# One x layout for both layers of the second block, and products of 512 columns issued as 256-column halves

## The chip, the cores and the metric

The kernel runs on one core of a Trainium2 chip. The metric is the device time of one execution in microseconds (us); smaller is better. Engines are named as the profile names them: PE is TensorE (PEld its weight loads), DVE is VectorE, ACT is ScalarE, POOL is GpSimd, SP is SyncE.

## The reference

Two transformer blocks, one behind the other, on 256 tokens of 1024 features in fp32. The first block (a recurrence with retention, a sparse attention, two feed-forward layers) is not touched in its code. The second block has two layers, and its first layer works on 512 rows: the 256 tokens of x ("now") and 256 tokens of a context. Its second layer takes the 256 tokens as queries and all 512 rows as keys. What the change touches is every product of the normed and modulated h with a weight matrix in these two layers:

```python
def _layer(x, xc, ...):
    h = _rms(x, norm_w) * (1.0 + sc[:, None, :]) + sh[:, None, :]
    hc = _rms(xc, norm_w) * (1.0 + sc_c) + sh_c
    aq, ak, av, az, dq, dk, dv, dz, bf, bz, cu, cv, cz = _split_in(h @ w_in)
    aqc, ... = _split_in(hc @ w_in)
    ...
    y = _merge(h, (o_a, o_d, o_b, o_c), (az, dz, bz, cz), w_br, w_merge, b_merge, w_out)

def _merge(h, outs, gates, w_br, w_merge, b_merge, w_out):
    yb = jnp.stack([o * jax.nn.silu(z) for o, z in zip(outs, gates)], axis=2)
    y = jnp.einsum('bnrw,rwd->bnrd', yb, w_br)
    g = jax.nn.sigmoid(h @ w_merge + b_merge).reshape(b, n, N_BRANCH, D_MODEL)
    return jnp.sum(g * y, axis=2) @ w_out
```

## The kernel before

**Products in three parts.** Each fp32 operand is kept as a high part of type float32r and a low part with the rest. A product of one 128 x 128 block of a weight with a block of h is three matmuls (`product`, L321): weight high by x high (L329), weight high by x low (L330), weight low by x high (L331). Each matmul instruction carries its own weight load, so three loads go with three matmuls, though the first two load the same block. A result tile of 128 features is a group of eight products, k = 0 to 7, accumulated in one PSUM bank of 512 fp32 columns: 24 matmuls. `features` (L333) issues such a group. `rows` (L341) issues the turned form, in which x is the loaded operand and 256 columns of the weight are streamed (L326 to L328).

**Where x lies.** `both` ("XX" in the profile) holds x high and x low, 4096 columns each (eight blocks k of 512 columns: NOW is 0 to 256, CTX is 256 to 512). There are two views of it. `XX0` (L146) has the high part at column 0 and the low part at column 4096. `XX` (L147) is "shifted": the high part starts at column HI = 48 and the low part 4096 + 64 columns behind it, at 4096 + LO with LO = 112. `XH` and `XL` are the two halves of the shifted view. The first block and layer 1 of the second block use the shifted view, layer 0 uses `XX0`. In front of `ring`, `X` and `arena` there are small unused tensors (L130, L140) that set where the large ones start.

```python
HI, LO = 48, 112
def shifted(v, n):
    return v[:, HI:HI + 2 * (n + LO - HI)].rearrange("p (s q) -> p s q", s=2)[:, :, 0:n]
```

**Who fills x.** `adapted_vector` (L436) and `adapted_scalar` (L454) apply the norm, gain and shift: ACT writes the high part, DVE the low part, 256 columns at a time.

**Layer 0** (`Layer`, L2026 and L2048: NT = 512 rows). Its PE program is a fixed order written out by hand:
- `context_keys_tensor` (L2154): the keys and values of the 512 rows, in groups of 256 columns (features of CTX and NOW, and turned products);
- `queries_tensor` (L2125) and `outer_tensor` (L2359): ten groups of 512 columns; `rest_tensor` (L2377): four turned groups of 256;
- `layer_tensor` (L2692): attention in 16 units, between whose steps `inner_tensor` (L2423) puts single groups of 512 columns (`product_of`, six of them) and, through `gate` (L2484), the first two gate groups, each in two pieces of four k;
- the merge, through `block` (L2722): 30 more gate groups of 512 columns, between them the branch products (`branches` in the profile, K = 2) of 512 columns; then the out products (`merged`) of 512 columns.

So there are 10 + 6 + 2 + 30 = 48 groups of 512 columns of x in layer 0.

**Layer 1** (NT = 256) streams 256 columns of x at a time, but for `all_keys_tensor` (L2135), whose two key groups take all 512 rows in one matmul each, from the shifted view.

**Weights** arrive by DMA (SP queue) in halves of 512 KB into `stage`, ACT copies them to the high part (`high`, L250), DVE takes the rest to the low part (`low`, L258); PE waits for a half in `Chunk.arrive` (L284). ACT waits with a chunk until PE is done with the chunk two before it. Sequence of chunks: `FLOW`, one fixed list.

Of the kernel before, what the change touches and what calls it, by code (L numbers as in the profile page):

```python
# [17 lines left out]
HI, LO = 48, 112  # L18
# [99 lines left out]
def build(nc, A, out):  # L118
    ctx = ExitStack()
    with ctx:  # L120
# [22 lines left out]
            return v[:, HI:HI + 2 * (n + LO - HI)].rearrange("p (s q) -> p s q", s=2)[:, :, 0:n]  # L143

        both = sb("XX", 8448, F32R)
        XX0 = both[:, 0:8192].rearrange("p (s k n) -> p s k n", s=2, k=8)  # L146
        XX = shifted(both, 4096).rearrange("p s (k n) -> p s k n", k=8)  # L147
        XH, XL = XX[:, 0], XX[:, 1]
        WH = [sb(f"WH{i}", 2048, F32R)[:, :] for i in range(2)]
# [52 lines left out]
        NOW, CTX = slice(0, 256), slice(256, 512)  # L202
# [118 lines left out]
        def product(e, dst, w, k, cols, xh, xl, start, stop, turned=False):  # L321
# [8 lines left out]
            e.matmul(dst, wh, xl, start=False, stop=False)  # L330
            return e.matmul(dst, wl, xh, start=False, stop=stop)  # L331

        def features(e, dst, w, c, name, x=None, xs=NOW, parts=(XH, XL)):  # L333

            for k in range(8):
                if x:
                    x(k)
                last = product(e, dst, w, k, slice(c, c + 128), parts[0][:, k, xs], parts[1][:, k, xs], k == 0, k == 7)
            last.then_inc(*pe.tick(name))

        def rows(e, dst, w, t, cols, name, x=None, base=0, parts=(XH, XL)):  # L341
# [92 lines left out]


        def adapted_vector(e, p, src, gain, shift, inv, t, xs, hold=None):  # L436
            x = (XX0, XX)[p[1] == "1"]

            def low(k):
                e.wait_ge(*ac.of(f"{p}.xh{k}"))  # L440
                e.scalar_tensor_tensor(out=x[:, 1, k, xs], in0=t[:, k, :], scalar=shift(k), in1=x[:, 0, k, xs].bitcast(F32),
                                       op0=ALU.add, op1=ALU.subtract).then_inc(*ve.tick(f"{p}.x{k}"))

            for k in range(9):
                if k < 8:
                    e.scalar_tensor_tensor(out=t[:, k, :], in0=src[:, k, :], scalar=gain(k), in1=inv, op0=ALU.mult,
                                           op1=ALU.mult).then_inc(*ve.tick(f"{p}.t{k}"))
                    if k == 7 and hold:
                        banks.emptied(hold, ve)
                if k > 0:  # L450
                    low(k - 1)
                yield

        def adapted_scalar(e, p, shift, t, xs):  # L454
            x = (XX0, XX)[p[1] == "1"]
            for k in range(8):
                e.wait_ge(*ve.of(f"{p}.t{k}"))
                e.activation(x[:, 0, k, xs], t[:, k, :], ACT.Identity, bias=shift(k)).then_inc(*ac.tick(f"{p}.xh{k}"))
                yield
# [1563 lines left out]
        class Layer:  # L2023
            def __init__(self, l):
                self.l = l
                self.NT = 512 if l == 0 else 256  # L2026
                self.nt, self.NZ = self.NT // 128, 2 * self.NT
                self.Z = view(0, 8 * self.NT, "p (r a n) -> p r a n", r=4, a=2)
                a = self.tail = 8 * self.NT
                self.R = [view(a + 1536 * n, 1536, "p (a n) -> p a n", a=3) for n in range(2)]  # L2030
                self.V = view(a + 3072, 1024, "p (t b c) -> p t b c", t=4, b=2)
                a += 4096
                self.S3 = [view(a + 1536 * n, 1536, "p (a n) -> p a n", a=3) for n in range(2)]
                self.T3 = [view(a + n, 768, "p (a n) -> p a n", a=3) for n in (3072, 4864)]
                self.RX = [view(a + 3840 + 512 * n, 512, "p (t h d) -> p t h d", t=4, h=2) for n in range(2)]
                self.S = [view(a + 1024 * n, 1024) for n in range(3)]
                self.T = [view(a + 3072 + 1024 * n, 1024) for n in range(2)]

                self.ms, self.rs = [SM[:, 24 * n:24 * n + 24] for n in range(2)], [SM[:, 48 + 24 * n:72 + 24 * n] for n in range(2)]
                d, NZ = C("decay"), self.NZ  # L2040
                self.U = d[:, 0:NZ].rearrange("p (a n) -> p a n", a=2)
                self.VT = d[:, NZ:2 * NZ].rearrange("p (t c) -> p t c", t=self.nt)
                self.Fm = self.U
                self.ZZ = d[:, NZ:NZ + 512].rearrange("p (t a c) -> p t a c", t=2, a=2)
                self.nsink = MOD[:, 96:100]
                NT = self.NT
                self.M = view(4096, 8 * NT, **eight)
                x, hi, lo = (XX0, 0, 0) if l == 0 else (XX, HI, LO)  # L2048
                self.x = x[:, 0], x[:, 1]
                self.MH, self.ML = [v[:, at:at + 8 * NT].rearrange("p (k n) -> p k n", k=8) for v, at in ((mh, hi), (ml, lo))]  # L2050
                self.SG, self.T2 = [[d[:, NT * (2 * i + n):NT * (2 * i + n + 1)] for n in range(2)] for i in range(2)]
                z = [v[:, at:at + w * NT].rearrange("p (r a n) -> p r a n", r=w // 2, a=2)
                     for v, w, at in ((zh, 8, hi), (zl0, 4, lo), (zl1, 4, lo))]

                self.ZH, self.ZL = [z[0][:, i] for i in (1, 0, 2, 3)], [z[1 + i // 2][:, i % 2] for i in range(4)]
                self.units, self.at = [], []

                self.steps = ([1] * 18 + [0], [2, 1, 2, 2, 1, 2, 1, 1, 2, 1, 0])[l]
                sink, nsink = [v.rearrange("p (q h) -> p q h", q=2) for v in (P("sink", l * 4, 4), self.nsink)]
                for br in range(2):  # L2060
                    for it in range(self.nt):
                        for h in range(2):
                            k0 = 0 if it < 2 else 256
                            rate = self.rs[br][:, 8 + 4 * it + 2 * h:10 + 4 * it + 2 * h].rearrange("p (q h) -> p q h", q=2)
                            self.units.append(Unit(1, 512 - k0, 512, rate,
                                                   (causalM, beforeM)[it] if br == 1 and it < 2 else None, 128 * (1 - it),
                                                   (sink[:, :, h:h + 1], nsink[:, :, h:h + 1]) if br else None))
                            self.at.append((br, it, h, k0))
# [354 lines left out]
        def inner_tensor(e, flow, rings, L):  # L2423
            l, NT, nt, s = L.l, L.NT, L.nt, (6, 7)
            w = {}
# [58 lines left out]
            def gate(m, ks):  # L2484
# [3 lines left out]
                    tile(e, f"g{l}.{m}.0", 1, (5,)) if l + m == 0 else tile(e, f"g{l}.{m}.0", 2, (0, 2))  # L2488
                b = banks[f"g{l}.{m}.0"]
                for k in ks:  # L2490
                    t = product(e, b[:, 0:NT], w["merge"], 8 * m + k, slice(0, 128), L.x[0][:, k, 0:NT], L.x[1][:, k, 0:NT], k == 0,
                                k == 7)
                if ks[-1] == 7:
                    t.then_inc(*pe.tick(f"g{l}.{m}.0"))
                    if m == 1:
# [5 lines left out]
            wsp, n = ring_take(e, rings, 512, "p (g q) -> p g q", g=4)  # L2501
# [190 lines left out]
        def layer_tensor(e, flow, rings, L):  # L2692
# [29 lines left out]
            def block(dst, xh, xl, k, K, name):  # L2722
                nonlocal w, n
                if n % 16 == 0:
                    w = Chunk(flow, f"merge_{l}", n // 16, 16)
                t = product(e, dst, w, n % 16, slice(0, 128), xh, xl, k == 0, k == K - 1)
                if k == K - 1:
                    t.then_inc(*pe.tick(name))
                elif n % 16 == 15:
# [470 lines left out]
```

## Time and profile before

| what | value |
|---|---|
| time of three runs, median (lowest to highest) | 1361.29 us (1360.18 to 1363.97) |
| the profiled execution's own time | 1365.15 us |
| its span, first to last instruction | 1363.3 us |
| granted TensorE clock, mean | 1.000 |
| PE busy | 1344.2 us, 99% of the span, 10306 matmuls |
| PEld busy | 1200.5 us, 88%, 10306 weight loads |
| DVE, ACT, POOL busy | 790.6, 640.8, 160.1 us (58%, 47%, 12%) |
| chain that ended last | PE 88%, DVE 7%, ACT 3%, issue 1%, DMA 1% |

The page gives busy time by engine, the chain of work that ended last, and groups of instructions by line. Matmuls are pipelined: the duration of one (276 ns for 256 columns, 389 ns for 512) is longer than the distance from its start to the next start, which is what it costs. That distance is read from start times in the timeline, or from a stretch that holds nothing else: in it the profile counts the matmuls that touch the stretch, so that one costs (length + one duration) / count.

### The profile page before, as it was taken

To read this page: it belongs to the slowest core of one execution; us is meant where nothing else is said; L and a number is where in the kernel's file an instruction comes from. 1 tells how busy PE (TensorE), PEld (TensorE's weight loads), DVE (VectorE), ACT (ScalarE), POOL (GpSimd) and SP (SyncE) were. 2 spreads that over 40 slices of the span, in tenths; PEclk is the share of its full clock that TensorE was granted. 3 is DMA by queue.
4 is the path that set the end of the run, shared out by engine and by line. 5 is a ranking of instruction groups with operands and counts; after the bars stand their busy time and mean duration, and the time that the engine had idled before them with its cause. 6 is when DMAs were issued, how large, how long until landed. Compare 5 with 4: busy or idle time off the path is not lost.

```text
span 1363.3 us, 24540 instructions
## 1 busy us (share of the span) xinstructions
PE 1344.2 (99%) x10306; PEld 1200.5 (88%) x10306; DVE 790.6 (58%) x1239; ACT 640.8 (47%) x1126; POOL 160.1 (12%) x131
## 2 busy tenths in 40 slices
PE   9999999999999999999999999999999999999999
PEld 8989999999855899999987777888888888879999
DVE  6976666557767666655724567433333455775554
ACT  6645444444365554455433445323232345555442
POOL 0020111001300012110004000111011100301110
PEclk9999999999999999999999999999999999999999
DMA  8535767556597455665432210222222234414553
GB/s 319 186 124 185 229 226 256 188 186 217 186 336 267 150 190 191 199 197 173 140 115 94 93 56 32 93 93 93 93 93 95 92 122 144 147 61 153 194 186 124
DMA packets 60974, 215.43 MB, mean 158 GB/s; under 512 B 6720, under 2 KB 12736, under 8 KB 57408
## 3 DMA queue, kind: packets, MB, share of 16 engines
q1 hardware_dynamic: 56272, 206.59, 45.4%
q10 hardware_dynamic: 4592, 7.26, 1.5%
q8 instruction: 82, 1.34, 0.4%
q14 instruction: 28, 0.23, 0.1%
HBM read 208.59 MB, written 1.05 MB: 154 GB/s over the span
## 4 chain that ended last, share of the span: by engine, by line
PE 88%; DVE 7%; ACT 3%; issue 1%; DMA 1%; SPq 0%; POOL 0%; ACTq 0%; DVEq 0%; POOLq 0%
PE psum L329 24%; PE psum L330 23%; PE psum L331 23%; DVE WL L261 3%; PE psum L1246 3%; PE psum L1271 2%; PE psum L1409 2%; PE psum L326 1%; PE psum L327 1%; PE psum L328 1%; ACT WH L256 1%; PE psum L2714 1%; PE psum L1602 1%; DMA stage<-ab_in 1%; PE psum L1250 1%
## 5 line engine op out<-in xcount | busy, mean ns | idle before, releaser
L329 PE MATMUL psum<-XX,WH 128*128 128x256 f32 (+1 forms) x1912 | 584.7, 306 | 8.2 <-DVE WL L261 2.8
L331 PE MATMUL psum<-XX,WL 128*128 128x256 f32 (+1 forms) x1912 | 576.3, 301 | 0.0
L330 PE MATMUL psum<-XX,WH 128*128 128x256 f32 (+1 forms) x1912 | 576.3, 301 | 0.0
L261 DVE TENSOR_TENSOR WL<-stage,WH 128x1024 fp32r<-128x1024 f32 x332 | 397.1, 1236 | 254.9 <-ACT WH L256 254.7
L256 ACT ACTIVATE WH<-stage 128x1024 fp32r<-128x1024 f32 x332 | 333.4, 1052 | 330.1 <-PE psum L331 286.0
L329 PEld LDWEIGHTS psum<-XX,WH 128*128 128x128 f32 x1912 | 359.4, 188 | 39.7 <-issue 13.8
L331 PEld LDWEIGHTS psum<-XX,WL 128*128 128x128 f32 x1912 | 359.9, 188 | 15.9
L330 PEld LDWEIGHTS psum<-XX,WH 128*128 128x128 f32 x1912 | 358.8, 188 | 15.7 <-issue 0.5
L329 PE MATMUL psum<-hidden,WH 128*128 128x256 f32 x352 | 97.5, 277 | 0.0
L331 PE MATMUL psum<-hidden,WL 128*128 128x256 f32 x352 | 97.2, 276 | 0.0
L330 PE MATMUL psum<-hidden,WH 128*128 128x256 f32 x352 | 97.2, 276 | 0.0
L2883 POOL TENSOR_TENSOR arena<-arena,con 128x512 f32<-128x512 f32 (+1 forms) x48 | 43.0, 895 | 385.6 <-DVE con L2801 385.0
L1371 ACT ACTIVATE arena<-psum,SM 128x16 f32<-128x16 f32 (+3 forms) x144 | 67.6, 482 | 2.3 <-DVE SM L1303 2.3
L329 PEld LDWEIGHTS psum<-hidden,WH 128*128 128x128 f32 x352 | 66.1, 188 | 0.4 <-issue 0.4
L330 PEld LDWEIGHTS psum<-hidden,WH 128*128 128x128 f32 x352 | 66.1, 188 | 0.0
L331 PEld LDWEIGHTS psum<-hidden,WL 128*128 128x128 f32 x352 | 66.1, 188 | 0.0
L1197 POOL TENSOR_TENSOR arena<-arena,SM 128x512 f32<-128x512 f32 x22 | 42.6, 1936 | 182.1 <-ACT arena L1164 182.1
L1356 ACT ACTIVATE arena<-psum 128x512 f32<-128x512 f32 (+2 forms) x48 | 32.9, 685 | 61.8 <-PE psum L1271 57.0
L2801 DVE TENSOR_TENSOR con<-psum,con 128x512 f32<-128x512 f32 (+1 forms) x48 | 26.3, 555 | 57.8 <-ACT con L2641 29.8
L2641 ACT ACTIVATE con<-psum,par 128x512 f32<-128x512 f32 (+1 forms) x64 | 35.6, 574 | 43.9 <-PE psum L331 43.9
L1300 DVE TENSOR_REDUCE SM<-psum 128x2 f32<-128x1024 f32 (+4 forms) x48 | 41.8, 872 | 20.2 <-PE psum L1246 12.2
L326 PE MATMUL psum<-WH,XX 128*128 128x256 f32 x176 | 49.9, 283 | 0.4 <-DVE WL L261 0.4
(288 smaller groups left out, 1675.7 us busy)
## 6 DMA issues: line engine op xcount, KB each, us to landing
stage<-w SPq DMA_DIRECT2D x132, 512.0 KB, 4.6
stage<-merge SPq DMA_DIRECT2D x80, 512.0 KB, 4.5
ring<-ada SPq DMA_DIRECT2D x24, 1024.0 KB, 7.0
stage<-in SPq DMA_DIRECT2D x44, 512.0 KB, 4.5
stage<-ab_in SPq DMA_DIRECT2D x22, 512.0 KB, 5.8
stage<-nsa_in SPq DMA_DIRECT2D x20, 512.0 KB, 4.8
stage<-out SPq DMA_DIRECT2D x16, 512.0 KB, 4.2
stage<-ab_out SPq DMA_DIRECT2D x8, 512.0 KB, 4.7
```

What stands on the lines that cost most here:

```text
L256: e.activation(hi, raw, ACT.Copy).then_inc(s_hi, 1)
L261: e.tensor_tensor(lo, raw, hi.bitcast(F32), ALU.subtract).then_inc(s_lo, 1)
L326: e.matmul(dst, xh, wh, start=start, stop=False)
L329: e.matmul(dst, wh, xh, start=start, stop=False)
L330: e.matmul(dst, wh, xl, start=False, stop=False)
L331: return e.matmul(dst, wl, xh, start=False, stop=stop)
L1197: e.tensor_tensor(F.sg[c % 3], F.sg[c % 3], spread(RT, 2, 256), ALU.mult).then_inc(*gp.tick(f"{p}.gate{c}"))
L1246: t = e.matmul(v[:, q, h, :], query(h)[r], key[r], start=h == 0 or u.mask is None, stop=u.mask is None)
L1300: e.tensor_reduce(nm, scored(p, n, u), AX.X, ALU.max, negate=True).then_inc(*ve.tick())
L1371: e.activation(s[:, q, h, :], v[:, q, h, :], ACT.Exp, bias=nm[:, q, h:h + 1], scale=rate, accum_out=sm[:, q, h:h + 1]).then_inc(*ac.tick(f ...
L2641: e.activation(L.SG[n % 2], banks[f"g{l}.{m}.{i}"][:, 0:L.NT], ACT.Sigmoid, bias=P("b_merge", l * 32 + MERGED[i] * 8 + m)).then_inc(*ac.ti ...
L2883: e.tensor_tensor(L.M[:, m, :], L.M[:, m, :], L.T2[n % 2], ALU.add).then_inc(*gp.tick(f"u{l}.{n}"))
```

## The change

`XX0` goes away: layer 0 of the second block keeps x in the shifted view, like the rest of the program. Groups of 512 columns of x go through a new function, `by_halves`. It issues the first matmul of a group (k = 0, weight high by x high) and the last (k = 7, the same operands) with 512 columns; all others are issued as three for the NOW half and three for the CTX half (at k = 0 and k = 7 two for each, since the third is the wide one). A group is then 46 matmuls in place of 24: 2 of 512 columns and 44 of 256. It is used wherever 512 columns of x are streamed: in the 48 groups of layer 0 and in the two key groups of layer 1. The products of `branches` and of `merged` keep their addresses and their 512 columns. The last matmul of a group signals its end, as before.

```diff
         both = sb("XX", 8448, F32R)
-        XX0 = both[:, 0:8192].rearrange("p (s k n) -> p s k n", s=2, k=8)
         XX = shifted(both, 4096).rearrange("p s (k n) -> p s k n", k=8)
...
+        def by_halves(e, dst, w, at, cols, k):
+            wh, wl = w.hi[:, at, cols], w.lo[:, at, cols]
+            w.arrive(e, at)
+            if k == 0:
+                e.matmul(dst, wh, XH[:, k, 0:512], start=True, stop=False)
+            for v in (NOW, CTX):
+                if 0 < k < 7:
+                    e.matmul(dst[:, v], wh, XH[:, k, v], start=False, stop=False)
+                e.matmul(dst[:, v], wh, XL[:, k, v], start=False, stop=False)
+                t = e.matmul(dst[:, v], wl, XH[:, k, v], start=False, stop=False)
+            if k == 7:
+                t = e.matmul(dst, wh, XH[:, k, 0:512], start=False, stop=True)
+            return t
...
         def features(e, dst, w, c, name, x=None, xs=NOW, parts=(XH, XL)):
+            both = parts[0] is XH and xs.stop - xs.start == 512
             for k in range(8):
                 if x:
                     x(k)
-                last = product(...)
+                if both:
+                    last = by_halves(e, dst, w, k, slice(c, c + 128), k)
+                else:
+                    last = product(...)
...
         def adapted_vector(e, p, src, gain, shift, inv, t, xs, hold=None):
-            x = (XX0, XX)[p[1] == "1"]
+            x = XX
...
         def adapted_scalar(e, p, shift, t, xs):
-            x = (XX0, XX)[p[1] == "1"]
+            x = XX
...
-                x, hi, lo = (XX0, 0, 0) if l == 0 else (XX, HI, LO)
-                self.x = x[:, 0], x[:, 1]
+                hi, lo = (0, 0) if l == 0 else (HI, LO)
+                self.x = XH, XL
...
             def gate(m, ks):
-                    t = product(e, b[:, 0:NT], w["merge"], 8 * m + k, ...)
+                    if NT == 512:
+                        t = by_halves(e, b[:, 0:NT], w["merge"], 8 * m + k, slice(0, 128), k)
+                    else:
+                        t = product(e, b[:, 0:NT], w["merge"], 8 * m + k, ...)
...
             def block(dst, xh, xl, k, K, name):
-                t = product(e, dst, w, n % 16, slice(0, 128), xh, xl, k == 0, k == K - 1)
+                if K == 8 and NT == 512:
+                    t = by_halves(e, dst, w, n % 16, slice(0, 128), k)
+                else:
+                    t = product(e, dst, w, n % 16, slice(0, 128), xh, xl, k == 0, k == K - 1)
```

## Rows read from the trace of the kernel before

**Rows 1.** The page: the chain of waits by engine.

```profile
PE 88%; DVE 7%; ACT 3%; issue 1%; DMA 1%; SPq 0%; POOL 0%; ACTq 0%; DVEq 0%; POOLq 0%
```

**Rows 2.** Stretches of one kind of matmul (engine: busy us, xcount of instructions).

```profile
core 0: us, PE busy (x) PEld busy (x) DVE busy (x) ACT busy (x) POOL busy (x), PEclk, DMA share, GB/s
500.00:600.00 100.00, 100.00 (x885) 100.00 (x884) 62.07 (x73) 46.58 (x64) 19.83 (x10) 1.00 0.59 193
672.00:689.00 17.00, 17.00 (x144) 17.00 (x143) 10.76 (x26) 8.01 (x14) 0.00 (x0) 1.00 0.11 38
900.00:1050.00 150.00, 150.00 (x664) 124.20 (x663) 49.27 (x53) 44.77 (x55) 20.06 (x18) 1.00 0.30 99
1137.00:1146.50 9.50, 9.50 (x43) 7.59 (x42) 5.66 (x11) 7.49 (x13) 0.00 (x0) 1.00 0.42 142
1240.00:1340.00 100.00, 100.00 (x851) 100.00 (x850) 52.79 (x68) 48.48 (x71) 18.81 (x28) 1.00 0.58 189
```

**Rows 3.** Groups by form, 663 to 1113 us, PE (xcount | busy, mean ns | idle).

```profile
L329 PE MATMUL psum<-XX,WH 128*128 128x512 f32 x384 | 151.3, 394 | 0.0
L331 PE MATMUL psum<-XX,WL 128*128 128x512 f32 x384 | 149.6, 390 | 0.0
...
L326 PE MATMUL psum<-WH,XX 128*128 128x256 f32 x64 | 18.1, 283 | 0.0
...
L329 PE MATMUL psum<-XX,WH 128*128 128x256 f32 x32 | 9.3, 291 | 0.0
```

**Rows 4.** Groups by form, 1126 to 1175 us, PE.

```profile
L329 PE MATMUL psum<-XX,WH 128*128 128x512 f32 x16 | 6.3, 395 | 0.0
```

**Rows 5.** Chain of waits, 774 to 777 us (start us, us, what).

```profile
774.85 0.87 PE psum L1271 x8
```

**Rows 6.** Timeline of PE, first stretch at shifted addresses, 15 us (start us, us).

```profile
14.63 0.39 PE L329 MATMUL psum<-XX,WH 128*128 128x256 f32 x1 [0.77 <-DVE WL L261]
14.85 0.28 PE L330 MATMUL psum<-XX,WH 128*128 128x256 f32 x1
...
16.78 0.28 PE L329 MATMUL psum<-XX,WH 128*128 128x256 f32 x1
```

**Rows 7.** Timeline of PE behind two transposes, 1160 us (start us, us).

```profile
1160.06 0.37 PE L329 MATMUL psum<-XX,WH 128*128 128x256 f32 x1
1160.27 0.28 PE L330 MATMUL psum<-XX,WH 128*128 128x256 f32 x1
...
1161.18 0.28 PE L329 MATMUL psum<-XX,WH 128*128 128x256 f32 x1
```

**Rows 8.** Timeline of PE behind a wait, 317 us.

```profile
316.69 0.36 PE L329 MATMUL psum<-XX,WH 128*128 128x256 f32 x1
316.88 0.28 PE L330 MATMUL psum<-XX,WH 128*128 128x256 f32 x1
...
317.83 0.28 PE L329 MATMUL psum<-XX,WH 128*128 128x256 f32 x1
```

**Rows 9.** Timeline of PE behind attention scores, layer 0, 777 us.

```profile
776.71 0.50 PE L329 MATMUL psum<-XX,WH 128*128 128x512 f32 x1
777.05 0.40 PE L330 MATMUL psum<-XX,WH 128*128 128x512 f32 x1
...
778.66 0.39 PE L331 MATMUL psum<-XX,WL 128*128 128x512 f32 x1
```

**Rows 10.** Timeline of PE, start of layer 1's merge, 1230 us.

```profile
1230.15 0.39 PE L329 MATMUL psum<-branches,WH 128*128 128x256 f32 x1
1230.37 0.28 PE L330 MATMUL psum<-branches_low,WH 128*128 128x256 f32 x1
...
1231.31 0.28 PE L329 MATMUL psum<-branches,WH 128*128 128x256 f32 x1
```

**Rows 11.** Waits of PE, 663 to 1113 us (us in total, times, longest).

```profile
PE psum L1901 <- DVE SM L1927: 0.6, 1, 0.6
PE psum L2458 <- DVE arena L2775: 0.2, 1, 0.2
```

More of the change, by code:

```diff
@@ L337, in features @@
                     x(k)
-                last = product(e, dst, w, k, slice(c, c + 128), parts[0][:, k, xs], parts[1][:, k, xs], k == 0, k == 7)
+                if both:
+                    last = by_halves(e, dst, w, k, slice(c, c + 128), k)
+                else:
+                    last = product(e, dst, w, k, slice(c, c + 128), parts[0][:, k, xs], parts[1][:, k, xs], k == 0, k == 7)
             last.then_inc(*pe.tick(name))
@@ L2490, in gate @@
                 for k in ks:
-                    t = product(e, b[:, 0:NT], w["merge"], 8 * m + k, slice(0, 128), L.x[0][:, k, 0:NT], L.x[1][:, k, 0:NT], k == 0,
-                                k == 7)
+                    if NT == 512:
+                        t = by_halves(e, b[:, 0:NT], w["merge"], 8 * m + k, slice(0, 128), k)
+                    else:
+                        t = product(e, b[:, 0:NT], w["merge"], 8 * m + k, slice(0, 128), XH[:, k, NOW], XL[:, k, NOW], k == 0, k == 7)
                 if ks[-1] == 7:
```

## The prediction

> **What bounds the kernel now.** I read the chain of waits first. PE carries 88% of the chain that ended last [rows 1], and the three lines of `product` are nearly all of that, so what counts is the distance from one matmul's start to the next. In layer 0 of the second block PE waits for other engines 0.8 us in 450 us [rows 11]: nothing hides a longer product, and nothing eats a shorter one. The granted clock is 1.00, the level of 2.4 GHz, in every stretch read [rows 2]; PE's work stays as dense after the change, so I change nothing there. DMA is busy 0.30 of the time in the merge, ACT 45 and DVE 49 us of 150 [rows 2]: weights are no bound, now or at 5% either way.
>
> Then I took stretches that hold only one kind of matmul and divided. Length plus one duration, over the count, gives [rows 2]:
> - 256 columns, shifted, 500 to 600 us (feed-forward): 100.28/885 = 113.3 ns;
> - 256 columns, shifted, 1240 to 1340 us (merge of layer 1): 100.28/851 = 117.8 ns;
> - 256 columns, unshifted, 672 to 689 us: 17.28/144 = 120.0 ns;
> - 512 columns, unshifted, 900 to 1050 us (merge of layer 0): 150.39/664 = 226.5 ns;
> - 512 columns, shifted, 1137 to 1146.5 us (keys of layer 1): 9.89/43 = 230 ns; one matmul fewer in the count would make 235, and I take 233.
>
> Two things are to be seen. A 512-column matmul at `XX0`'s addresses costs exactly two of the fast 256-column ones (2 x 113.3 = 226.6). And at shifted addresses the same instruction has two levels, 113.3 and 117.8, each of them kept for 100 us and more. Which one a stretch takes is set at its start, behind an interruption: eight steps from 1160.27 take 0.91 us (114) [rows 7], eight from 316.88 take 0.95 us (119) [rows 8], eight from 1230.37 take 0.94 us (118), and that one keeps the slow level through the merge of layer 1 [rows 10, 2]. I counted the stretches of at least 12 such matmuls at shifted addresses: 50, from the first at 15 us (17 steps in 1.93 us, 114 ns) [rows 6] to the last at 1230 us [rows 10]; 26 end at the fast level and 24 at the slow one. I see no line, operand or half of x that goes with either. So for a stretch in a new place it is close to a coin.
>
> What makes the 256-column form cost over 106.7 ns (256 columns at 2.4 GHz) is most likely its weight load: eight transposes of only 128 columns, each with a load, take 0.87 us, 109 ns each [rows 5], although they stream half as much, and PEld is busy in the whole of both 256-column stretches but in 124 of 150 us beside 512 columns [rows 2].
>
> **The change, part by part.**
>
> 1. Groups of layer 0. 384 matmuls of 512 columns by each of three lines [rows 3], that is 1152/24 = 48 groups, each 24 x 226.6 = 5438 ns. After: 44 halves and 2 wide ones. The wide ones are now shifted: 233 each, 466 (bounds 226.6 and 235). The halves: at the fast level 44 x 113.3 = 4985, the group 5451, **+13 ns**, +0.6 us in 48 groups. At the slow level 44 x 117.8 = 5183, the group 5649, **+211 ns**, +10.1 us. Below, the nearest row is the 109 ns of a 128-column matmul: 44 x 109 = 4796, the group 5262, -176 ns, -8.4 us. No row shows a 256-column product under 113.3, so this is the bound and not the value. I take the fast level: in a group the halves follow a wide matmul, whose 233 ns leave its successor's load done long before, so that they start without a late load, and that is how the two longest stretches (feed-forward) run on; but this is the weak step.
>
> 2. Entry into a group. A 512-column stretch behind the attention's matmuls needs some steps to settle: seven steps from 777.05 take 1.61 us, 230 each in place of 226.6, and the first takes 0.34 us [rows 9]. 18 groups of layer 0 lie there. After, the first step is wide again and as dear, and only two wide steps are left to be unsettled; the halves cost 0.5 to 1 ns over for some eight steps [rows 7]. 18 x (24 to 50 ns) saved against 48 x (0 to 20 ns) spent: zero, bounds -0.9 and +1.0 us.
>
> 3. The 256-column products of layer 0 (keys, values, turned ones): 64 by each of L326 to L328, 32 by each of L329 to L331 [rows 3], 288 together, unshifted at 120.0, shifted at 113.3 or 117.8: -1.9 or -0.6 us, I take the middle, **-1.3 us**.
>
> 4. The two key groups of layer 1, 16 matmuls by each line [rows 4]: 24 x 233 = 5592 before, 5451 or 5649 after: **-0.3 us** or +0.1.
>
> 5. 50 x 22 = 1100 more matmuls and loads. The price of a load is in the distances above. Instruction fetch: no row of layer 0 shows PE waiting for it, and the 256-column stretches already issue at this rate. Zero. No wait is added or moved; ACT and DVE write x in the same order at the new columns, zero as well, hidden as before by PE's work.
>
> Here a page speaks against the change. The Trainium skill, "TensorE: Matmul & The Clock Gate", section "Back-to-back issue gap", gives 262 cycles for 256 columns and 518 for 512, a fixed cost of about 2.5 ns for each matmul. By it a split costs 2.5 ns: an estimate from that page is 50 x 22 x 2.5 ns = 2.8 us slower, 1363. The trace doesn't agree: it shows 2 x 113.3 against 226.5, no fixed cost to be saved by width.
>
> Sum: +0.6 + 0 - 1.3 - 0.3 = -1.0 us. The profiled execution took 1365.15 us with a span of 1363.3, the median of the runs is 1361.29 and they spread over 3.8 us; two levels that differ by 4.5 ns in the some 1100 matmuls of layer 1's merge alone (851 in 100 us, and it lasts 130 us: 4.9 us) can make such a spread. I put the -1.0 to the median: **1360.3 us**. A measurement of this kernel can tell about 0.3%, 4.1 us, from no change.
>
> **The rivals.**
>
> - *The halves run at the slow level.* Place: the 48 groups of layer 0. For it: 24 of 50 stretches, and the stretch nearest in kind, layer 1's merge, which starts out of a row of attention matmuls and mixes x and branch products [rows 10, 2]. Against it: both feed-forward stretches, 100 us and more at 113.3. Price: +10.1 - 0.6 + 0.1 = +9.6, so 1370.9 us. It decides from where the mean of the 2112 halves passes 113.3 + (4.1 + 1.0) us/2112 = 115.7 ns. Chance 0.25.
> - *Each group falls to a level of its own*, since two wide matmuls interrupt the halves in every group. Half of them slow: +5.3 - 1.3 - 0.1 = +3.9, so 1365.2 us. Chance 0.15, evenly on both sides of the 0.3%.
> - *Faster, the halves under 113.3.* Two halves behind one wide matmul could run nearer to the load's own 109 ns [rows 5]: -8.4 - 1.3 - 0.6 = -10, 1351 us. Against it: no stretch of 256 columns does. Chance 0.10.
> - *Faster, layer 1 gets the fast level.* Its merge starts afresh behind attention; 1100 products by 4.5 ns are -4.9 us, with the forecast -5.9, so 1355.4 us. For it: that level is taken at a start, and the starts will fall otherwise. Against it: the spread of the runs suggests that this coin is thrown in every run, so that the median has it in already. Chance 0.13.
> - *The change does nothing at all* (the forecast without its small gains, 1361.3) can't be told from the forecast and shares its chance, 0.37 together.
>
> **How the numbers follow.** Same: 0.37 and half of 0.15, 0.44. Faster by over 0.3%: 0.10 + 0.13 = 0.23, and a little for bounds of both: 0.24. Slower by over 0.3%: 0.25 + 0.07 = 0.32. The range must take the slow level in at one end, 1371, and at the other the case of layer 1, with part of the way to the load's bound: 1353. The likeliest case's own range, from the bounds of terms 1 to 4, is 1358 to 1363.
>
> **What would show it.** In the profile after: 11406 matmuls; no 512-column matmul on XX but 100 (two in each of 50 groups). In a stretch of layer 0's merge, a group of gates plus its branch products takes 5451 + 6 x 226.6 = 6811 ns if the forecast holds, 7009 at the slow level, against 6798 before. The stretch from 672 to 689 us should show 113.3 or 117.8 and not 120. PE's weight loads should be busy nearly all of the merge, not 0.83 of it. The forecast is wrong if the halves' mean distance lies above 115.7 or under 112, or if waits of PE for weights (DVE, L261) turn up in layer 0.

## The result and the profile after

| | before | after |
|---|---|---|
| median of the first comparison (4 runs each) | 1361.85 us | 1369.62 us (1368.41 to 1372.2) |
| ratio, 95% interval | | 1.005 [1.0029, 1.0071] |
| second comparison (26 and 10 runs) | 1367.07 us | 1368.52 us, 0.9999 [0.9974, 1.0024] |
| third comparison (23 and 12 runs) | 1367.43 us | 1370.67 us, 1.0022 [0.9999, 1.0045] |
| span of the profiled execution, again, a third time | 1363.3, 1363.3 us | 1366.6, 1367.8, 1363.3 us |

The forecast was 1360.3 us, 1.0 us less than before. In the first comparison the changed kernel is slower, by 0.3 to 0.7%, and the other two can't tell it from no change. By how much it is slower, the medians tell badly (7.8, 1.5 and 3.2 us); the profiles tell it well. From the last matmul on `hidden` (the input of the feed-forward layer's second product, the last work of the first block) to the first on `early` (the input of layer 1's first products), a stretch that is layer 0 and a few us around it, the kernel before takes 444.7 us in both of its profiles, the changed one 448.3, 448.5 and 448.7: **+3.6 to +4.0 us**. Two executions, 1480.1 us of the kernel before and 1658.4 us with the addresses alone, ran at a mean granted clock of 0.85 and 0.75 and are in no ratio.

The engines' busy time and the chain of waits, from the page of the changed kernel:

```profile
PE 1347.2 (99%) x11406; PEld 1247.5 (91%) x11406; DVE 790.8 (58%) x1239; ACT 641.0 (47%) x1126; POOL 160.0 (12%) x131
...
PE 88%; DVE 7%; ACT 3%; issue 1%; DMA 1%; SPq 0%; POOL 0%; ACTq 0%; DVEq 0%; POOLq 0%
```

1100 matmuls and loads more, PEld at 91% of the span in place of 88, and the chain as before [rows 1]: the change did what it says, and PE bounds the kernel as it did.

Groups by form, 663 to 1117 us, PE (xcount | busy, mean ns of one | idle):

```profile
L341 PE MATMUL psum<-XX,WH 128*128 128x256 f32 x768 | 207.0, 278 | 0.0
...
L340 PE MATMUL psum<-XX,WH 128*128 128x256 f32 x576 | 160.7, 279 | 0.0
L328 PE MATMUL psum<-branches,WH 128*128 128x512 f32 x64 | 25.2, 394 | 0.0
...
L337 PE MATMUL psum<-XX,WH 128*128 128x512 f32 x48 | 20.1, 418 | 0.0
L344 PE MATMUL psum<-XX,WH 128*128 128x512 f32 x48 | 18.8, 391 | 0.0
L325 PE MATMUL psum<-WH,XX 128*128 128x256 f32 x64 | 17.9, 279 | 0.0
```

In layer 0, 48 groups with a wide matmul at the start (L337), one at the end (L344), and 44 halves (768 + 768 + 576 = 2112 in all) stand where three lines had 384 wide ones each [rows 3] (L342, with 768 as well, is left out above). The branch products are the same 192, but their mean duration went up from 389 to 391 ns to 392 to 394.

Stretches of the changed kernel (engine: busy us, xcount):

```profile
core 0: us, PE busy (x) PEld busy (x) DVE busy (x) ACT busy (x) POOL busy (x), PEclk, DMA share, GB/s
673.00:689.00 16.00, 16.00 (x142) 16.00 (x141) 10.35 (x25) 7.20 (x12) 0.00 (x0) 1.00 0.05 16
...
900.00:1050.00 150.00, 150.00 (x1130) 142.73 (x1129) 49.27 (x53) 44.11 (x54) 19.98 (x18) 1.00 0.28 96
1236.00:1336.00 100.00, 100.00 (x852) 100.00 (x851) 55.22 (x71) 49.06 (x72) 16.78 (x25) 1.00 0.56 188
```

Divided as before (length plus one duration, over the count), 673 to 689 gives 16.28/142 = 114.6 ns where the unshifted addresses gave 120.0 [rows 2]: this part of the change works. In the merge, the timeline over three neighbouring groups (start us, us; L337 is the first matmul of a group, L344 its last) shows what the groups cost:

```profile
865.54 0.39 PE L337 MATMUL psum<-XX,WH 128*128 128x512 f32 x1
...
870.96 0.39 PE L344 MATMUL psum<-XX,WH 128*128 128x512 f32 x1
871.19 0.39 PE L328 MATMUL psum<-branches,WH 128*128 128x512 f32 x1
...
872.57 0.39 PE L337 MATMUL psum<-XX,WH 128*128 128x512 f32 x1
872.80 0.28 PE L341 MATMUL psum<-XX,WH 128*128 128x256 f32 x1
...
878.03 0.39 PE L328 MATMUL psum<-branches,WH 128*128 128x512 f32 x1
...
879.41 0.39 PE L337 MATMUL psum<-XX,WH 128*128 128x512 f32 x1
...
886.44 0.39 PE L337 MATMUL psum<-XX,WH 128*128 128x512 f32 x1
```

From the first wide matmul at 872.57 to the next group's at 879.41 are 6.84 us, a gate group and six branch matmuls. The group before it began at 865.54 and took 7.03 to 872.57, and so does the one behind it (879.41 to 886.44). The expected values were 6811 ns for a fast group and 7009 for a slow one, against 6798 before. So **both levels are there, by turns**: the 30 groups of the merge take 5.457 and 5.648 us alternately, without one exception, and all three profiles show the same order. Behind a slow group the closing wide matmul takes 233 ns, behind a fast one 226 (870.96 to 871.19: 0.23). From the first branch product to the first on `merged` the merge takes 210.9 us in all three profiles, before 206.9 in both.

Where the 4.0 us of the merge go, from the distances of all its matmuls: the halves of 15 slow groups, 15 x 44 x 4.4 ns = 2.9; the halves of the 15 fast groups, 0.2 us over 113.3 while they settle; 60 wide x products at 231.1 in place of 226.7, 0.3; and 192 branch products, whose addresses and width didn't change, at 230.7 in place of 227.6, 0.6.

### The profile page after: what moved, and what is told of

Read it like the earlier page. It is cut to its first block, busy times and chain, and to the rows that moved or that the text cites. A ratio compares the mean times of both kernels' runs of the same rounds, so it can differ in the third digit from the quotient of the medians.

```text
span 1366.6 us, 26740 instructions
## 1 busy us (share of the span) xinstructions
PE 1347.2 (99%) x11406; PEld 1247.5 (91%) x11406; DVE 790.8 (58%) x1239; ACT 641.0 (47%) x1126; POOL 160.0 (12%) x131
## 4 chain that ended last, share of the span: by engine, by line
PE 88%; DVE 7%; ACT 3%; issue 1%; DMA 1%; SPq 0%; POOL 0%; ACTq 0%; DVEq 0%; POOLq 0%
PE psum L328 17%; PE psum L329 17%; PE psum L330 17%; PE psum L341 7%; PE psum L342 7%; PE psum L340 5%; DVE WL L260 3%; PE psum L1264 3%; PE psum L1289 2%; PE psum L1427 2%; PE psum L325 1%; PE psum L327 1%; PE psum L326 1%; ACT WH L255 1%; PE psum L2734 1%
## 5 line engine op out<-in xcount | busy, mean ns | idle before, releaser
L328 PE MATMUL psum<-XX,WH 128*128 128x256 f32 x1512 | 427.0, 282 | 8.4 <-DVE WL L260 3.4
L329 PE MATMUL psum<-XX,WH 128*128 128x256 f32 x1512 | 419.9, 278 | 0.0
L330 PE MATMUL psum<-XX,WL 128*128 128x256 f32 x1512 | 419.9, 278 | 0.0
L328 PEld LDWEIGHTS psum<-XX,WH 128*128 128x128 f32 x1512 | 284.0, 188 | 19.3 <-issue 10.0
L330 PEld LDWEIGHTS psum<-XX,WL 128*128 128x128 f32 x1512 | 284.9, 188 | 0.0
L329 PEld LDWEIGHTS psum<-XX,WH 128*128 128x128 f32 x1512 | 283.6, 188 | 0.5 <-issue 0.5
L341 PE MATMUL psum<-XX,WH 128*128 128x256 f32 x800 | 215.6, 278 | 0.0
L342 PE MATMUL psum<-XX,WL 128*128 128x256 f32 x800 | 215.4, 278 | 0.0
L340 PE MATMUL psum<-XX,WH 128*128 128x256 f32 x600 | 167.4, 279 | 0.0
L342 PEld LDWEIGHTS psum<-XX,WL 128*128 128x128 f32 x800 | 150.3, 188 | 2.2
L341 PEld LDWEIGHTS psum<-XX,WH 128*128 128x128 f32 x800 | 150.3, 188 | 1.5
L340 PEld LDWEIGHTS psum<-XX,WH 128*128 128x128 f32 x600 | 113.6, 189 | 1.2 <-issue 1.2
```

The lines of the kernel that those rows point to most:

```text
L328: e.matmul(dst, wh, xh, start=start, stop=False)
L340: e.matmul(dst[:, v], wh, XH[:, k, v], start=False, stop=False)
L341: e.matmul(dst[:, v], wh, XL[:, k, v], start=False, stop=False)
L342: t = e.matmul(dst[:, v], wl, XH[:, k, v], start=False, stop=False)
```

## The experiments

All start from one of the two kernels. "Merge" is the time from layer 0's first branch product to its first on `merged`; before 206.9, after 210.9. "Layer 0" is from the last matmul on `hidden` to the first on `early`; before 444.7, after 448.3 to 448.7. "Tail" is from layer 1's first branch product to the end of the span; before 133.1 twice, after 133.1, 133.1 and 128.3. "Fast" and "slow" are the two levels, 113.3 and 117.8 ns for 256 columns at shifted addresses. A train is a row of halves without a wide matmul in it; the wide ones or the 256-column ones settle when their distances have come down to an even value after an interruption.

### Both kernels again

> The kernel before, unchanged, for a second profile. Theory A (the level of a stretch of 256-column products follows from the fixed order of PE's instructions in front of it): the stretches show the same levels as in the first profile where PE waits for nobody, feed-forward layers 113.3 ns, layer 1's merge 117.8 ns. Theory B (a coin thrown in every run): some of the long stretches change sides, by 5 to 7 us each for a feed-forward layer and 4.9 us for layer 1's merge. Time 1361.9 us either way.

> The changed kernel, unchanged, for a second profile. In its first profile the 30 gate groups of layer 0's merge take 5.457 and 5.648 us by turns, without one exception. Theory A (a cycle set by the order of the instructions): the same alternation again, the mean of the halves 115.3 ns. Theory B (coin): another pattern, and halves anywhere between 113.3 and 117.8. The time should be 7 to 8 us over that of before; 3.3 us of it are seen in the spans of the first profiles, so the second pair should show where the other 4 are.

> The changed kernel once more, since its two timed comparisons disagree (1.005 and 0.9999) while its two profiles agree (+3.3 and +4.5 us in the span). If the profiles have it right, the ratio lies near 1.003 and the alternation of 5.46 and 5.65 us stands in the merge a third time; layer 0 from its first wide product to the start of layer 1 takes 421 us.

Measured: before again has a span of 1363.3 us, layer 0 444.7, tail 133.1; 0.9998 [0.9974, 1.0021] against itself. The changed kernel again: 1367.8, layer 0 448.5, tail 133.1, and a third time 1363.3, layer 0 448.7, tail 128.3. Theory A holds in the merge, where PE waits for nobody: the same turns three times. Theory B holds where PE restarts behind another engine: stretches at 15 and 323 us change sides between the two profiles of before, and in the third profile of the changed kernel layer 1's merge came out fast, 100.28/885 = 113.3 ns:

```profile
1236.00:1336.00 100.00, 100.00 (x885) 100.00 (x884) 57.90 (x74) 52.37 (x76) 16.79 (x25) 1.00 0.57 190
```

That is 4.8 us, which is why this one execution has the span of the kernel before. Medians of a few runs carry such throws. They don't touch layer 0's merge. In the ten profiles here in which layer 1's merge has no matmul added, it is fast in three: this one, the halves alone and no wide matmul at all.

### The addresses alone

```diff
         def by_halves(e, dst, w, at, cols, k):
-            wh, wl = w.hi[:, at, cols], w.lo[:, at, cols]
-            w.arrive(e, at)
...
-            return t
+            return product(e, dst, w, at, cols, XH[:, k, 0:512], XL[:, k, 0:512], k == 0, k == 7)
```

> Layer 0's x at the shifted addresses, its 512-column products left whole. If the addresses alone make a 512-column product dear (233.3 ns as in layer 1's keys against 226.6), 1152 matmuls cost 7.7 us more, the 288 of 256 columns save 0.6 to 1.9: 1361.9 + 6.4 = 1368.3 us. If the dear ones in layer 1 came from what stands in front of them there, the matmuls settle at 226.6 and the time is 1360.6 us.

Measured: 1.0046 [1.0026, 1.0066], layer 0 451.6 us (+6.9), merge 212.3. The stretch from 900 to 1050 us:

```profile
900.00:1050.00 150.00, 150.00 (x647) 120.65 (x646) 46.31 (x50) 42.71 (x53) 20.12 (x18) 1.00 0.28 92
```

150.39/647 = 232.4 ns, with the branch products in it; the 720 x products alone have a mean distance of 233.3. So at the shifted addresses a 512-column product is dear on its own, here behind x products and branch products alike. This is what the halves have to make good.

### The halves alone

The changed kernel with `XX0` back for layer 0 (in `adapted_vector`, `adapted_scalar`, `self.x` and as an argument of `by_halves`).

> Layer 0's x at the old addresses, its 512-column products as 44 halves and 2 wide ones. If 256 columns at these addresses always cost 120.0 ns, a group takes 44 x 120.0 + 2 x 226.6 = 5733 ns in place of 5438, 48 groups +14.2 us: 1376.0 us, with no levels and no alternation. If the two wide matmuls in a group break that up, the groups lie between 5.44 and 5.73 us.

Measured: 1.0069 [1.0036, 1.0102], layer 0 458.5 us (+13.8), merge 216.3.

```profile
900.00:1050.00 150.00, 150.00 (x1097) 142.84 (x1096) 46.33 (x51) 42.93 (x54) 20.23 (x18) 1.00 0.28 96
```

150.39/1097 = 137.1 ns a matmul, the halves 119.8 in all 30 groups. One level, no turns. The turned products of layer 0, in which x is the loaded operand and the weight is streamed, keep to 120.0 as well, as in the kernel before, and come to 113.3 or 117.8 with x shifted: the pace goes with the addresses of x in either role. So each part of the change alone is a loss, 6.9 and 13.8 us; together they lose 3.6 to 4.0, and with the merge at the fast level, as the next two runs show, 1.6 to 2.5.

### One wide matmul in place of two

```diff
-                if 0 < k < 7:
+                if 0 < k:
...
-                t = e.matmul(dst[:, v], wl, XH[:, k, v], start=False, stop=False)
-            if k == 7:
-                t = e.matmul(dst, wh, XH[:, k, 0:512], start=False, stop=True)
+                t = e.matmul(dst[:, v], wl, XH[:, k, v], start=False, stop=k == 7 and v is CTX)
```

> The changed kernel with only the first matmul of a group wide; k = 7 is issued as six halves like the others. Theory A1: what sets the level is the state at the group's start, which comes from the branch products, so the turns stay, and layer 0 takes 421 us. Theory B: one of two interruptions is gone; between groups that follow each other the level would then be kept from the former one, and the pattern changes.

Measured: one execution, 1368.97 us beside 1368.45 for before; merge 207.9, layer 0 447.2, tail 133.1.

```profile
900.00:1050.00 150.00, 150.00 (x1166) 143.56 (x1165) 49.28 (x53) 44.78 (x55) 19.68 (x19) 1.00 0.28 94
```

All 30 groups of the merge are fast, halves at 113.6. Theory A1 expected the turns to stay; theory B said only that the pattern would change. Between two trains of halves there are now seven wide matmuls, six of branches and one of x, where there were eight (one, six, one), and with that the turns are gone. Outside the merge this edit makes it worse: of the 18 groups ahead of it 12 are slow, where the changed kernel has 5 or 6. Where group follows group, a single wide matmul now stands between two trains, and behind the fast group at 691 us come three slow groups; with two wide ones there, all four are fast. That is why layer 0 loses 2.5 us though the merge loses 1.0. The starts of three groups in a row, 5.45 and 5.65 us apart:

```profile
691.08 0.39 PE L337 MATMUL psum<-XX,WH 128*128 128x512 f32 x1
...
696.53 0.39 PE L337 MATMUL psum<-XX,WH 128*128 128x512 f32 x1
...
702.18 0.40 PE L337 MATMUL psum<-XX,WH 128*128 128x512 f32 x1
```

### The branch products in pairs

```diff
                     for m in (2 * c, 2 * c + 1):
                         if c + i > 0:
                             b = tile(e, f"g{l}.{m}.{i}")
...
+                    for m in (2 * c, 2 * c + 1):
                         b = tile(e, f"y{l}.{m}.{i}")
...
```

The blocks of the merge weights are laid out in the same order.

> The changed kernel with the merge in another order: two gate groups, then the two branch products together (12 wide matmuls in a row, in place of 6 after each group). In both profiles of the changed kernel the groups of layer 0's merge take turns, 5.457 and 5.648 us. Theory A1 (the six wide branch matmuls are too few to settle: behind a slow group they leave the next one fast, behind a fast one slow): with 12 in a row they settle at 226.7, and the gate groups come out fast, 5.453 each, as the five at 689 to 711 us that follow one another do; layer 0 from its first wide product to the start of layer 1 takes 421.2 - 2.9 = 418.3 us, the span 1363.5 to 1365. Theory B (the wide matmuls at k = 0 and 7 throw each group's level anew): a mixture again, 421 us.

Measured: merge 208.0 us, layer 0 446.3, all 30 groups fast.

```profile
900.00:1050.00 150.00, 150.00 (x1143) 142.54 (x1142) 49.83 (x53) 45.09 (x56) 21.33 (x19) 1.00 0.27 94
```

The level is the one that A1 named, but its reason is only half right: the twelve branch matmuls take 230.2 ns each on average and not 226.7; the last two of them are down to 227. Between trains there are now either two wide matmuls or fourteen. The span of this execution is 1368.7 us for two reasons outside: a clock drop at 370 to 390 us (below) and the tail, 133.7, with a step of 1.3 us in the `merged` products.

### No wide matmul at all

```diff
-            if k == 0:
-                e.matmul(dst, wh, XH[:, k, 0:512], start=True, stop=False)
             for v in (NOW, CTX):
-                if 0 < k < 7:
-                    e.matmul(dst[:, v], wh, XH[:, k, v], start=False, stop=False)
+                e.matmul(dst[:, v], wh, XH[:, k, v], start=k == 0 and v is NOW, stop=False)
```

The last wide matmul goes too, as above.

> The changed kernel with no wide matmul in a group: 48 halves, the first alone with the start flag. If the wide ones are what makes a group's level, the groups now all have one level, 48 x 113.3 = 5.438 us (layer 0 then takes 417.5 us) or 48 x 117.8 = 5.654 us (428 us). If the branch products set it, they take turns as before, 5.44 and 5.65, 422 us.

Measured: merge 213.3 us, layer 0 451.6.

```profile
900.00:1050.00 150.00, 150.00 (x1160) 145.10 (x1159) 46.31 (x50) 42.81 (x53) 20.30 (x19) 1.00 0.27 94
```

All 30 groups slow, 117.8, and the branch products between them at 226.7 from their first one on. With the two runs before: in the merge the fast level comes behind a wide matmul **at shifted addresses** right in front of the halves, when the branch products ahead of it had settled; straight from six unshifted branch products they go slow each time. The cycle of the changed kernel, from its distances: behind a slow group the six branch matmuls take 226, 236, 228, 232, 231 and 227 ns, so they have settled, and the next group starts fast; behind a fast group they take 229, 229, 233, 236, 224 and 231, the next wide one 232, and the next group starts slow. With one wide matmul less they take 232, 232, 231, 227, 226 and 227 behind a fast group. That the settling is the cause, and not a thing that goes along with it, isn't shown.

The profiles of the changed kernel and of the two runs before hold more cases, in which wide matmuls of x and no wait stand between two rows of at least twelve 256-column products. Two wide ones were followed by the fast level in all 28 cases behind a fast row and in 10 of 11 behind a slow one (as at 1144.52 us in the changed kernel); the eleventh lies in its third profile, ten matmuls behind a step of 213 ns. A single one was followed by the slow level in 8 of 10 cases behind a slow row (as at 1139.10 us) and in 5 of 8 behind a fast one; the five others all stand behind turned products. The changed kernel's two key groups in layer 1 show both, a single wide one behind a slow row and then a pair:

```profile
1139.10 0.40 PE L337 MATMUL psum<-XX,WH 128*128 128x512 f32 x1
1139.34 0.28 PE L341 MATMUL psum<-XX,WH 128*128 128x256 f32 x1
...
1144.52 0.39 PE L344 MATMUL psum<-XX,WH 128*128 128x512 f32 x1
1144.75 0.39 PE L337 MATMUL psum<-XX,WH 128*128 128x512 f32 x1
1144.98 0.28 PE L341 MATMUL psum<-XX,WH 128*128 128x256 f32 x1
...
1149.98 0.39 PE L344 MATMUL psum<-XX,WH 128*128 128x512 f32 x1
```

The 44 halves take 5.18 us in the first, 117.7 ns each, and 5.00 in the second, 113.6 with the settling.

### Layer 1's merge: more steps at its start

In the kernel before: one 256-column matmul more, or two, or one of 512 columns on XX, ahead of the first branch product of layer 1. The next product overwrites the result. The first of the three:

```diff
                     w = Chunk(flow, f"merge_{l}", n // 16, 16)
+                if l == 1 and n == 16:
+                    w.arrive(e, 0)
+                    for _ in range(1):
+                        e.matmul(dst, w.hi[:, 0, 0:128], xh, start=True, stop=True)
```

> The kernel before with one more 256-column matmul at the start of layer 1's merge, whose result the next one overwrites. In both profiles of before, and of the changed kernel, this merge runs at 117.8 ns to its end; in two other kernels, whose layer 0 differs, it runs at 113.3. If the level is set by the state at the start alone, one more matmul can move it: the stretch of 1102 matmuls takes 124.9 in place of 129.8 us, the span 1358.5. If not, the span is 1363.4.

> The kernel before with two more 256-column matmuls at the start of layer 1's merge. One more left it at 117.8 ns. If the number of steps decides (each shifts the phase between loads and matmuls), two may give 113.3: layer 1 from its first branch product to the end 129 us in place of 133.2. If only what stands before the start decides, 133.3.

> The kernel before with one more 512-column matmul, at shifted addresses, at the start of layer 1's merge. In the changed kernel, groups that start wide behind the attention's value products came out fast in 8 of 10 cases of both profiles (at 805, 817, 838, 849 us and so on). If that carries over, the merge runs at 113.3: 129.3 us from the first branch product to the end, span 1359.5. If not, 133.4 and 1363.6.

Measured: tails 132.5, 133.3 and 132.2 us; in all three the merge stays at the slow level. The start with two more, by the timeline:

```profile
1230.86 0.50 PE L2729 MATMUL psum<-branches,WH 128*128 128x256 f32 x2
...
1231.32 0.28 PE L330 MATMUL psum<-branches_low,WH 128*128 128x256 f32 x1
```

Three misses: the level did not turn. Three steps from 1230.86 to 1231.32 take 0.46 us, the first, behind the attention's last matmul, 0.23 and the other two 0.114 and 0.118, and the stretch then goes on at 117.8, as it does without the two. The 0.6 and 0.9 us gained in two of them come from the `merged` products behind the merge, from whose first to the end it takes 24.8 us in place of 25.6. They go on slow and turn fast at the 22nd, with no recorded wait. The first of these runs' reasons was off as well: of the two other kernels in which layer 1's merge was said to be fast, the runs shown up to then have one, the halves alone. The cases on which I had built the third (counted again, 7 of 10 and not 8) don't carry over.

### Layer 1's merge: two wide matmuls inside

```diff
                 if n % 16 == 0:
                     w = Chunk(flow, f"merge_{l}", n // 16, 16)
+                if l == 1 and n == 18:
+                    for _ in range(2):
+                        e.matmul(banks["y1.1.0"], w.hi[:, 2, 0:128], XH[:, 0, 0:512], start=True, stop=True)
                 t = product(e, dst, w, n % 16, slice(0, 128), xh, xl, k == 0, k == K - 1)
```

> The kernel before with two more 512-column matmuls at shifted addresses in layer 1's merge, behind its first six products and not at its start (their result is overwritten). In both profiles of the changed kernel a slow group, a wide matmul at its end and a wide one behind it were followed by a fast group, each time (at 731, 743 and 1145 us in the first). If the level is a state that such a pair turns over, the rest of the merge runs at 113.3: from the first branch product to the end 133.2 + 0.5 - 4.7 = 129.0 us, the span 1359.1, and against the runs of before 0.3% faster. If not, 133.7 us and 1363.8.

Measured: **0.9967 [0.9952, 0.9983]**, median of 12 runs 1361.75 us beside 1367.43. Tail 129.6 us in place of 133.1, in spite of two matmuls more. The timeline at the place (start us, us):

```profile
1239.47 0.28 PE L330 MATMUL psum<-branches_low,WH 128*128 128x256 f32 x1
1239.59 0.28 PE L331 MATMUL psum<-branches,WL 128*128 128x256 f32 x1
1239.70 0.63 PE L2728 MATMUL psum<-XX,WH 128*128 128x512 f32 x2
1240.17 0.28 PE L329 MATMUL psum<-branches,WH 128*128 128x256 f32 x1
...
1241.09 0.28 PE L331 MATMUL psum<-XX,WL 128*128 128x256 f32 x1
```

1239.47 to 1239.59 is a slow step. The two wide ones (x2) run from 1239.70 to 1240.17, and from there eight steps take 0.92 us (115 with the settling). So the level turned at the pair and not at the start of the merge, which began slow; by the cases above one wide matmul would not have done, but no run put a single one, or another pair of matmuls, in this place. Two stretches of the same kernel:

```profile
250.00:300.00 50.00, 50.00 (x427) 50.00 (x426) 26.13 (x32) 22.89 (x30) 0.00 (x0) 1.00 0.58 189
1242.00:1342.00 100.00, 100.00 (x885) 100.00 (x884) 57.29 (x74) 50.29 (x73) 17.25 (x26) 1.00 0.60 193
```

The second is layer 1's merge: 100.28/885 = 113.3 ns; before it was 117.8 [rows 2]. The pair brings 3.6 us of the expected 4.2, since not all of the `merged` products behind the merge are gained: the 22nd of them takes 207 ns, and from there they are slow. Such a step of 205 to 207 ns stands there in all four profiles with a fast merge, and in one of the ten with a slow merge (the branch products in pairs) a longer one, of 1.3 us, just before. The first is in feed-forward layer 0, at 50.28/427 = 117.8 where all my other profiles have 113.3: in this one execution its throw fell badly. Its span, 1368.5, says nothing on the edit for that reason, and the 12 runs do: 7 of them lie below 1362 us, one of 22 of the kernel before.

## Why the prediction was wrong

**What bounds the kernel, the distances, the term for the addresses.** Right. 120.0, 226.6 and 233 ns came back in every kernel that had such matmuls in such a place, and the two parts of the change, each alone, were costed at +6.4 and +14.2 us before they ran; layer 0 measured +6.9 and +13.8.

**Step 1, groups of layer 0: this failed.** "I take the fast level: in a group the halves follow a wide matmul, whose 233 ns leave its successor's load done long before". The reason is refuted: every group starts that way, and in the merge half of them are slow. The level goes with what came before the wide matmul. The measured term is +2.9 us for the 15 slow groups of the merge, +0.5 there for the wide ones and the settling, and about +1.0 to 1.2 for five or six slow groups ahead of the merge, and not +0.6 for all 48. I had found that the levels are set at starts, and then treated every start as a coin. Behind a wait they can be one: the group at 804 us, behind attention, is fast in two profiles and slow in the other. Inside PE's own order they are fixed, and the three profiles agree on all 30 groups of the merge.

The sign that I had set for this, a mean distance of the halves above 115.7 ns, would have missed it: all 2112 halves have 115.6 in the first profile, those of the merge 115.7. A mean halfway between the levels is what turns look like. The weight loads were busy for 142.7 of 150 us in the merge, as expected.

**The rival "each group falls to a level of its own"** is what happened, at 1365.2 us by its price and +3.9; +3.6 to +4.0 are measured in layer 0. It had 0.15. It was wrong on the kind, since in the merge there are turns and no throws, and the close size is in part luck: 20 or 21 of 48 groups are slow and not 24, and the small products saved less than it took, while the branch products cost 0.6 that it left out. The slow-level rival (+9.6) and the one with halves near 109 ns are both out: no half ran under 113.3 in the mean of a settled group.

**Step 2, entry into a group,** zero with bounds of -0.9 and +1.0: within them, but a part was missing. The branch products were left out as untouched; standing between halves they have to settle anew each time, 192 x 3.1 ns = 0.6 us. From layer 0's first wide matmul to its first branch product, the attention with it, 166.3 to 166.4 us became 166.8 to 166.9: what was saved on settling is less there than what the slow groups cost.

**Step 3, the small products,** -1.3 us: from the last `hidden` product to layer 0's first wide one 27.9 us before, 27.1 to 27.6 after, -0.8 to -0.4; the stretch at 673 us ran at 114.6, but others of these products, and in the third profile that one too, run at 118, so the size was too hopeful.

**Step 4, layer 1's keys,** -0.3 us: two groups took 11.3 us, now 11.2 in two profiles and 11.5 in the third, where steps of 213 and 127 ns stand inside them. **Step 5**, zero: PE's recorded waits in layer 0 are 1.0 us in place of 0.8, none of them for weights.

**The page on fixed cost per matmul** (the Trainium skill, "TensorE: Matmul & The Clock Gate", section "Back-to-back issue gap"). A fast group behind a 256-column product took 5.444 us (from 689.06), against 5.440 for 24 wide ones, so 22 more matmuls cost 4 ns in all. By the page's 2.5 ns each, which it gives for the isolated gap of a single matmul, it would be 55. But that sets narrow matmuls at shifted addresses against wide ones at unshifted, and so did the prediction's 2 x 113.3 against 226.5. At equal addresses two narrow ones against a wide one are 240.0 against 226.7 ns unshifted, and 226.6 or 235.6 against 233.3 shifted: +13.3, -6.7 or +2.3 ns. The measurement decides: in these fp32 products no one fixed cost shows, and which sign a split has depends on the addresses and the level.

**Layer 1 as a gain.** That "this coin is thrown in every run" was borne out by the profiles: 113.3 in one of three profiles of the changed kernel, in none of two of before. That the median has it in already is no more than likely. A merge that comes out slow can be turned on purpose, for 0.3%.

What stays open: what the two levels are in the hardware. The runs show that they go with the addresses of x (120.0 alone at unshifted ones, two levels at shifted ones; one pair of places each was tried) and with what stands in front of a stretch. That the weight load is the bound of the 256-column form was only argued, from the 109 ns of the transposes.

## What to carry to other kernels

Where matmuls follow one another without a wait, read distances from start to start in the trace, by group, and not means over a stage: a stage at 115.7 ns was two levels by turns, and only distances group by group show it. A split of wide matmuls must be costed at the new addresses *and* in the new neighbourhood, for itself and for the unchanged matmuls between; try one change in the order (here one wide matmul less, or the branches in pairs; the one helped the merge and hurt the groups ahead of it) before the split is judged. And look in the timeline for long stretches on the slower level: here two matmuls put inside the stretch, not at its start, won 3.6 us of layer 1, where the restructured layer 0 lost 3.6 to 4.0.

## What the runs showed of the hardware that I had not expected

- One stream of fp32 256-column products at fixed addresses has two paces, 113.3 and 117.8 ns, each kept for 100 us and more. Short trains between wide matmuls can fall into a cycle with period two. A pace can also turn inside a stream with no step over 123 ns: three profiles turn fast so at the 22nd of layer 1's `merged` products or just behind it.
- Two 512-column matmuls at shifted addresses inside a slow stream turned it to the fast pace; one more matmul of either width, or two narrow ones, at its start did not.
- 512 columns of x at shifted addresses cost 233.3 ns once settled, at unshifted 226.7; 256 columns are the other way round, 113.3 or 117.8 against 120.0.
- The granted clock fell in some executions for a few us in the sparse attention of the first block, in four of the 14 profiles. Two stretches of one of them, one 256-column matmul more ahead of layer 1's merge, then the same two of the kernel before, run again (PE busy, ..., PEclk, DMA):

```profile
370.00:380.00 10.00, 8.03 (x95) 4.75 (x91) 7.74 (x19) 4.99 (x27) 3.66 (x4) 0.87 0.88 331
380.00:390.00 10.00, 10.00 (x99) 5.55 (x91) 4.67 (x16) 4.55 (x24) 0.00 (x0) 0.79 0.82 314
```

```profile
370.00:380.00 10.00, 7.51 (x100) 4.35 (x93) 8.05 (x19) 4.98 (x27) 3.64 (x3) 1.00 0.95 376
380.00:390.00 10.00, 9.99 (x115) 5.74 (x116) 4.98 (x17) 6.43 (x30) 0.00 (x0) 1.00 0.90 343
```

Only the first fell, to a mean of 0.87 and then 0.79 of the 2.4 GHz, so to 1.2 GHz for part of either stretch. In the 5 us before the fall, 370 to 375 at 1.00, PE was busy for 4.3 us in it, 4.6 in the second, and 3.8 in the first profile of the kernel before, which didn't fall: these rows don't tell the ones that fall from the ones that don't. It cost the execution 2.3 us up to 392 us, 1.5 to 3.1 in the four. Together with the throws of the levels this is part of the spread of the runs; whether it is all of it isn't shown.
